# Smaller first pieces of memory features and weights, norm vectors on ScalarE's DMA queue, eleven matmuls of zeros at the start, memory rows fetched one piece later

## The reference, cut to what matters

```python
mn = rms_norm(mem, mem_norm_g)                 # mem: 256 x 2048
mk, mv = jnp.split(mn @ w_mem_kv, 2, axis=-1)  # w_mem_kv: 2048 x 1024
...
xn = rms_norm(h, attn_norm_g)
proj = xn @ w_in                               # the next, much larger product
```

## Time and profile before

| | |
|---|---|
| median of three runs | 2552.91 us |
| profiled execution, whole time | 2553.15 us |
| its span of instructions | 2551.3 us |
| TensorE busy | 2489.3 us, 98% |
| VectorE, ScalarE, GpSimd busy | 62%, 47%, 2% |
| mean HBM traffic | 192 GB/s |

### The profile page before, as it was taken

One profiled execution on the slowest core, in us unless ns is written; L12 is line 12 of the kernel. 1 busy time (PEld: TensorE's weight loads), 2 busy tenths in 40 slices (PEclk: granted clock), 3 DMA queues, 4 the chain that ended last, 5 costly groups with the idle time before them and its releaser, 6 DMA issues.

```text
span 2551.3 us, 31644 instructions
## 1 busy us (share of the span) xinstructions
PE 2489.3 (98%) x12038; PEld 2168.0 (85%) x12038; DVE 1570.5 (62%) x2007; ACT 1208.6 (47%) x1516; POOL 61.5 (2%) x56
## 2 busy tenths in 40 slices
PE   8999978999999999999999999999899999999998
PEld 7888867888888888888888788888788888888887
DVE  6555777656565656567555767766665555555557
ACT  6443454544444444445344445565554444444444
POOL 1000250000000000000000000000000000000000
PEclk9999989999999999999999999999899999999999
DMA  9776505666566656567564445585456666666664
GB/s 370 215 205 204 151 1 183 191 204 198 197 197 197 198 197 200 194 200 229 166 220 132 159 139 182 189 289 195 131 198 202 198 197 197 197 197 198 199 203 140
DMA packets 244526, 488.72 MB, mean 192 GB/s; under 512 B 11928, under 2 KB 13240, under 8 KB 243672
## 3 DMA queue, kind: packets, MB, share of 16 engines
q1 hardware_dynamic: 240576, 470.42, 57.0%
q0 software_dynamic: 3104, 11.79, 1.2%
q10 hardware_dynamic: 760, 5.34, 0.5%
HBM read 485.42 MB, written 2.10 MB: 191 GB/s over the span
## 4 chain that ended last, share of the span: by engine, by line
PE 92%; DVE 4%; ACT 2%; issue 1%; DMA 1%; SPq 0%; DVEq 0%; ACTq 0%
PE ps_a L2280 24%; PE ps_a L2281 24%; PE ps_a L2282 24%; PE ps_b L2282 5%; PE ps_b L2281 5%; PE ps_b L2280 5%; DMA raw<-in_w_mem_kv 1%; PE ps_b L2586 1%; DVE wlo L1284 1%; PE ps_b L2345 1%; PE ps_b L2660 0%; ACT whi L568 0%; PE ps_b L2650 0%; ACT prob L967 0%; PE ps_b L2675 0%
## 5 line engine op out<-in xcount | busy, mean ns | idle before, releaser
L1284 DVE TENSOR_TENSOR wlo<-raw,whi 128x1024 fp32r<-128x1024 f32 x872 | 1057.2, 1222 | 712.9 <-ACT whi L568 711.7
L568 ACT CAST whi<-raw 128x1024 fp32r<-128x1024 f32 (+1 forms) x880 | 911.3, 1045 | 1046.2 <-PE ps_a L2282 821.0
L2280 PE MATMUL ps_a<-whi,xhi 128*128 128x512 f32 x2016 | 772.3, 383 | 10.2 <-DVE wlo L1284 7.2
L2281 PE MATMUL ps_a<-wlo,xhi 128*128 128x512 f32 x2016 | 765.6, 380 | 0.0
L2282 PE MATMUL ps_a<-whi,xlo 128*128 128x512 f32 x2016 | 765.5, 380 | 0.0
L2280 PEld LDWEIGHTS ps_a<-whi,xhi 128*128 128x128 f32 x2016 | 381.9, 189 | 69.9 <-issue 11.8
L2282 PEld LDWEIGHTS ps_a<-whi,xlo 128*128 128x128 f32 x2016 | 382.0, 189 | 54.6
L2281 PEld LDWEIGHTS ps_a<-wlo,xhi 128*128 128x128 f32 x2016 | 382.2, 190 | 52.6
L2280 PE MATMUL ps_a<-whi,x2hi 128*128 128x512 f32 x640 | 246.0, 384 | 12.1 <-DVE wlo L1284 12.1
L2281 PE MATMUL ps_a<-wlo,x2hi 128*128 128x512 f32 x640 | 243.3, 380 | 0.0
L2282 PE MATMUL ps_a<-whi,x2lo 128*128 128x512 f32 x640 | 243.3, 380 | 0.0
(11 more groups left out here) (365 smaller groups left out, 2001.8 us busy)
## 6 DMA issues: line engine op xcount, KB each, us to landing
raw<-in_w_in SPq DMA_DIRECT2D x108, 1024.0 KB, 5.5
raw<-in_w_up SPq DMA_DIRECT2D x108, 1024.0 KB, 5.4
raw<-in_w_down SPq DMA_DIRECT2D x108, 1024.0 KB, 5.1
raw<-in_w_gate SPq DMA_DIRECT2D x44, 1024.0 KB, 5.2
raw<-in_w_out SPq DMA_DIRECT2D x16, 1024.0 KB, 5.1
raw<-in_w_mix_out SPq DMA_DIRECT2D x16, 1024.0 KB, 5.7
raw<-in_w_br_attn SPq DMA_DIRECT2D x8, 1024.0 KB, 5.1
raw<-in_w_br_pool SPq DMA_DIRECT2D x8, 1024.0 KB, 5.0
```

Of the source, the lines that this page charges most:

```text
L568: return nc.scalar.copy(o, i)
L1284: return V.tensor_tensor(wlo[:, q % 4], raw[:, c % SLOTS, 2 * j:2 * j + 2], whi[:, q % 4].bitcast(F32), ALU.subtract).then_inc(lo_done, 1)
L2280: mm(o, x0, m0, start=first and j == 0, stop=False)
L2281: mm(o, x0, m1, start=False, stop=False)
```

## The change

It touches only the start:

- `gains` moves from the head of SyncE's queue to the head of ScalarE's.
- The first 512 KB of `mem_t` come as two DMAs of 256 KB, the first of them at the head of SyncE's queue, with its own semaphore; between the two stands the first part of c0.
- c1 comes as two DMAs of 512 KB; q2 waits only for the first.
- GpSimd's fetch of `mem_rows` waits for the third part of `mem_t` in place of the second.
- The four semaphores of each row fetch become one, waited for once at 64.
- VectorE writes zeros into 384 columns of `stage_t` at the start, and TensorE runs eleven matmuls on them (128x128 weights, 256 columns, float32) into `ps_b` ahead of its first real wait.

```diff
+            sp.dma_start(mem_t[:, 0:2], a["mem_t"][:, 0:2]).then_inc(first_flat, 16)
-            sp.dma_start(gains[:], a["gains_t"]).then_inc(ld["gains"], 16)
-            turned_memory(0)
             sp.dma_start(raw[:, 0, 0:2], rows(w1["memkv"], 0, 2 * P, 0)).then_inc(ld["first"], 16)
+            sp.dma_start(mem_t[:, 2:4], a["mem_t"][:, 2:4]).then_inc(flat_loaded[0][0], 16)
             load(0, rows(w1["memkv"], 2 * P, 2 * P, 0), raw[:, 0, 2:4])
-            for k in range(1, 4):
+            turned_memory(1)
+            sp.dma_start(raw[:, 1, 0:2], rows(w1["memkv"], 4 * P, 2 * P, 0)).then_inc(ld["second"], 16)
+            load(1, rows(w1["memkv"], 6 * P, 2 * P, 0), raw[:, 1, 2:4])
+            for k in range(2, 4):
                 turned_memory(k)
                 load(k, rows(w1["memkv"], k * CK * P, CK * P, 0))
...
+            act.dma_start(gains[:], a["gains_t"]).then_inc(ld["gains"], 16)
             act.wait_ge(table_in, 1)
...
                 if q == 0:
                     act.wait_ge(ld["first"], 16)
+                elif q == 2:
+                    act.wait_ge(ld["second"], 16)
...
-                    for j in range(4):
-                        act.wait_ge(norm_loaded[2 if n == 4 else n][j], 16)
+                    act.wait_ge(norm_loaded[2 if n == 4 else n], 64)
...
-                act.wait_ge(flat_loaded[n][j // 2], 16)
+                act.wait_ge(first_flat if (n, j) == (0, 0) else flat_loaded[n][j // 2], 16)
...
-            pool.wait_ge(flat_loaded[0][1], 16)
+            pool.wait_ge(flat_loaded[0][2], 16)
             load_rows(0, mem_rows, "mem")
...
             V.memset(small[:, 252:254], 1.0).then_inc(table_in, 1)
+            V.memset(stage_t[:, 0, 0:S + P], 0.0).then_inc(zeroed, 1)
             dve.wait_ge(ld["gains"], 16)
...
+            pe.wait_ge(zeroed, 1)
+            for n in range(11):
+                mm(ps_b[:, 0:S], stage_t[:, 0, S:S + P], stage_t[:, 0, 0:S], start=True, stop=True)
+
             pe.wait_ge(gain_sb, 1)
             flat_tile(0, "memkv", (x2hi, x2lo))
```

More of the change, by code:

```diff
@@ L270, in hybrid_blocks_kernel @@
         hi_done, lo_done, pe_half, evicted = sem("hi_done"), sem("lo_done"), sem("pe_half"), sem("evicted")
-        ld = {n: sem(f"ld_{n}") for n in ("ident", "gains", "base", "gw2", "bias", "cmp", "gain", "first")}
-        gain_sb, table_in = sem("gain_sb"), sem("table_in")
+        ld = {n: sem(f"ld_{n}") for n in ("ident", "gains", "base", "gw2", "bias", "cmp", "gain", "first", "second")}
+        gain_sb, table_in, zeroed = sem("gain_sb"), sem("table_in"), sem("zeroed")
+        first_flat = sem("first_flat")
         flat_hi, flat_lo = sem("flat_hi"), sem("flat_lo")
@@ L527, in hybrid_blocks_kernel @@
         norms = [mem_rows, h, h, h, mix, h, h]
-        norm_loaded = [[sem(f"{n}_loaded{j}") for j in range(4)] for n in ("mem", "x", "mem2")]
+        norm_loaded = [sem(f"{n}_loaded") for n in ("mem", "x", "mem2")]
         QUADS = {}
@@ L1189, in load_rows @@
                     c = slice(j * NT, (j + 1) * NT)
-                    pool.dma_start(rows_[:, :, c], a[src][0].rearrange("(b p) d -> p b d", p=P)[:, :, c]).then_inc(norm_loaded[n][j], 16)
+                    pool.dma_start(rows_[:, :, c], a[src][0].rearrange("(b p) d -> p b d", p=P)[:, :, c]).then_inc(norm_loaded[n], 16)
             def load_flat(n, src):
```

## The result

| | before | changed |
|---|---|---|
| median of 21 runs | 2553.27 us | 2556.94 us |
| lowest to highest | 2551.2 to 2556.27 | 2554.01 to 2559.67 |
| ratio, 95% interval | | 1.0015, 1.0008 to 1.0022 |
| profiled execution | 2553.15 us | 2555.55 us |
| its span | 2551.3 us | 2553.7 us |

The changed kernel is 3.7 us slower (2.0 to 5.6 by the interval). The two profiled executions differ by 2.4 us.

The account below looks back on a forecast made before the run. TensorE, busy 98%, was taken as the bound, its opening gated by q11, released by c5 plus ScalarE work. Later q11 +0.5 and clock loss +1.5 gave +2.0 on 2552.9, rounded to 2555.0 us; range 2549.5 to 2558.5.

Parts of the forecast that it names:

- First start: Opening: earlier feature DMA and fewer bytes ahead of q0's weights start the first matmul at 9.1, 1.2 us earlier.
- Zeros: Opening: memset 0.4 us, eleven matmuls 2.4 to 4.7 us; full clock for q0 would save 2.0 us, a pause might undo it.
- Case D: Opening, q0: zeros do not raise the clock or it falls again; still 2555, chance inside the forecast's 0.47.
- Memory rows later: GpSimd's trigger moves from 10.81 to 14.1; c3 lands 3.2 us earlier at 23.4, q6 starts at 25.9.
- what c5 does: Ahead of q11: `x_t` bytes delay c5 from 31.6 to 32.5; q11 starts at 42.9, +0.5 us (−0.4 to +2.4).
- case C: DMA queues at 28.8 to 33 us: `x_t` falls into c5, 2555.3 to 2560.4 us; chance 0.18.
- What TensorE does meanwhile: Ahead of q11: idle 3.3 to 4.1 us, then half clock for 3.4 us, +1.5 us (0 to 3.4).
- Case A: Pause ahead of q11: same q11 start but no clock loss, without the 1.5 us, 2553.4 us; chance 0.23.
- Later: After q11: c7's delay of up to 1.9 us is covered at q14; the single semaphore and extra issues cost nothing.
- Case B: Opening: something other than c5 or the memory passes releases q11, TensorE keeps 4.5 us, 2548.5; chance 0.12, whole or part.

Follow-up runs that it names:

- rows_late_alone: The kernel before with only the memory-row fetches moved behind the third feature part; 2552.50 us against 2553.15 for before.
- one_semaphore_alone: The kernel before with only the semaphore part, one for the four fetches of each row load; 2553.26 us against 2552.99 for before.
- late_one_semaphore: The kernel before with late memory rows and one semaphore for each row load; 2556.31 us against 2552.99 for before.
- four_semaphores: The changed kernel with a semaphore for each of the four memory-row fetches again, still late; 2556.72 us against 2552.99 for before.
- four_x_later: four_semaphores with GpSimd's fetch of `x_t` held until q10 is cast; 2555.70 us against 2553.10 for before.
- no_zeros: The changed kernel without the memset and the eleven matmuls of zeros; 2555.90 us against 2553.15 for before.
- one_ahead_4k: rows_4k with q11 alone cast ahead of the sums over the memory rows, on ScalarE and VectorE; 2551.71 us against 2553.10 for before.
- rows_4k: The changed kernel with memory rows in four 512 KB pieces of 128 4 KB runs, not 256 2 KB runs; 2555.54 us against 2553.15 for before.
- rows_early: The changed kernel with the memory-row fetches behind the second feature part again; 2552.03 us against 2553.15 for before.
- two_ahead_four: four_semaphores with q11 and q12 cast ahead of the sums over the memory rows; 2558.06 us against 2552.99 for before.

## Why the prediction was right, and where its steps were not

**Forecast and range.** 2555.0 us and "same" were forecast; 2556.94 was measured, 3.7 us above before, where the sum had 2.0. What made the verdict come true is that the opening is a matter of 5 us in 2553; the step that carried the forecast's +0.5 us was wrong (below). The frame held: only q11 matters, the opening's gain is lost in front of it, and the idle TensorE pays again with its clock.

**First start.** 9.1 forecast, 8.96 found; cast of q0 6.6 and 6.51. Right. The move of `gains` was hidden, though not as argued: on ScalarE's queue they took 3.7 us to land in place of 2.0, ScalarE's first pass at 4.48 waited for them, and only because q0's weights came at 6.51 did this cost nothing.

**Zeros.** The price was wrong by two. The memset took 0.38 us, as assumed. Eleven matmuls stand in the trace as 22 records, and took 7.64 us, not 2.4 to 4.7. I had read the earlier trace rows as one record for one matmul of 256 float32 columns; the counts of the page (12060 matmuls against 12038) say two. They ended just ahead of 8.96, so there was none of the 3 us of pause that the prediction feared, and q0 ran at a spacing of 0.22. That is luck: at the price assumed they would have left a gap. Case D did not occur, and as its text said, the time would not have shown it.

**Memory rows later.** Trigger 14.1 forecast, first issue 14.48; c3 used at 24.12, at the edge of 22.4 to 24.1, and q6 at 26.57 where 25.9 was taken.

**The failed step: what c5 does.** I had q11 released by c5 at 32.5, delayed by `x_t`. In the trace c5 is there at 30.39, and q11 waits for the memory rows to 34.31. The prediction counted all four row fetches ahead of c5. In the changed kernel the fourth was issued at 25.88 and moved next to nothing before c5 was there (queues, 25 to 30.4 us):

```profile
q1 hardware_dynamic: 1010, 2.00, 100.8%
q0 software_dynamic: 29, 0.10, 5.0%
```

Its 0.52 MB at 0.39 per us are the 1.3 us by which c5 came ahead of the 31.6 that the prediction had for it without `x_t`. `x_t`, issued at 27.54, could no more fall into c5 than that fetch. The mistake stands in the part on later effects: the single semaphore was costed at nothing, as nine waits fewer on ScalarE, and the queue that issues the fetches was not looked at. The four runs with and without late rows and a shared semaphore (before, rows_late_alone, one_semaphore_alone, late_one_semaphore) show that the two together are the loss. The number came out near all the same (+0.5 forecast for q11, +1.29 found), because a c5 delayed as forecast and rows delayed as found release q11 at nearly the same time (42.9 and 43.73); that was luck. The mechanism of case C was found in another kernel alone, four_semaphores, and there four_x_later puts 0.6 to 0.9 us on it, hardly more than profiles differ by. (C's own bound for c3, 30.3 − 2.95 − 3.4, is 23.95, not 23.8.)

**What TensorE does meanwhile.** Pause of 3.3 to 4.1 us forecast, 3.97 found; clock at half for 3.4 us, +1.5 forecast, +1.68 found. Right, and in this profile it is the larger half of the loss. The pause of before that the prediction took as 0.4 us stands in the trace as 0.15.

**Case A**, that the pause costs no clock, is what no_zeros did behind 2.89 us. So a fall behind such a pause is not certain, and one profile of each kernel does not tell in how many executions it comes.

**Later.** No wait of TensorE at q12 to q20 that the trace lists, as forecast.

**Case B**, that the gain reaches the end, failed for the reason given. one_ahead_4k shows its premise from the other side: with q11 freed, 2.2 of the 4.5 us arrive at q16.

**What stays open.** The medians differ by 3.7 us, q16 by 2.97 in one profile of each. The 0.7 between is within the interval, and I have no run that separates it from the clock's behaviour later in the kernel. no_zeros widens the question: its q16 is 1.13 us later than before, and its median 2.75.

## What to carry to other kernels

Making the opening faster is worth what the first fixed chain behind it lets through: find the one instruction that everything before it has to pass (here q11, behind 8 us of ScalarE work), and either free it first or expect nothing. Time won in front of such a point turns into idleness, and on TensorE idleness can cost twice, since the clock may fall behind it. A semaphore can be part of a DMA queue's timing, as it was on GpSimd's here: before merging semaphores, look at when the issuing engine sends each fetch, and price a merge and a later trigger together, because each was free alone.

## What the runs showed of the hardware that I had not expected

- GpSimd's fourth fetch of 512 KB in 256 runs goes out when the first has landed if each has its semaphore (18.6 to 18.9 behind early rows, 21.3 to 21.7 behind late ones), and about 4 us later if they share one (22.7 to 22.9, and 25.7 to 26.6). Four fetches of the same size in 128 runs of 4 KB did not wait, with one semaphore (rows_4k, 14.41, all within 2.24 us) or four (`x_t`).
- A plain float32 matmul of 128 rows by 256 columns appears as two matmul records (22 for eleven). At full clock the records start 0.216 us apart. In the changed kernel twelve of the 22 start from 1.37 to 6.5 us, some 0.45 apart, and the other ten in the 2.4 us behind.
- A pause does not decide alone whether the clock falls. Behind 1.89 us (rows_4k), 2.17 (rows_early, ahead of q4), 3.07, 3.39 and 3.97 us it fell for 3.4 us; behind 1.51, 1.53, 1.69 to 1.80 (ahead of q6, in the changed kernel, rows_4k and one_ahead_4k) and 2.89 us (no_zeros) it did not. In the longest pauses it fell while TensorE was still idle, and for 6.8 us: at 41.85 in the pause of 4.27 us (39.16 to 43.43, four_semaphores) and at 50.2 in that of 5.89 (44.89 to 50.78, two_ahead_four). The stretch of rows_4k shows it, in the columns of the table by stretch:

```profile
41.72:42.90 1.18, 1.18 (x5) 1.05 (x6) 1.18 (x2) 1.18 (x2) 0.00 (x0) 1.00 1.02 382
42.95:46.30 3.35, 3.35 (x10) 2.59 (x9) 2.57 (x5) 1.40 (x4) 0.00 (x0) 0.50 1.03 384
```

  TensorE was back at work for 1.2 us before the clock fell. The clock's rise varies too. The same 22 records of zeros, begun at 1.36 to 1.37, took 6.45 us in four_semaphores, 6.95 in rows_early and 7.64 in the changed kernel, with TensorE busy throughout. The Trainium skill, TensorE: Matmul & The Clock Gate, says in its section What's actually happening that the number of matmuls a kernel runs before its clock rises varies from run to run; these durations agree with it.
